# Weighted sum of gathered V rows: from one 128x128 array to four 64x64 tiles, two gathers at a time

## What is computed

```python
def block(xb):                                   # PEER_HEADS 8, PEER_TOPK 16, 16384 experts, D 1024
    ...
    best, sel = lax.top_k(cand, PEER_TOPK)
    eidx = jnp.take_along_axis(cidx, sel, axis=-1)
    gate = jax.nn.softmax(best, axis=-1)
    act = jax.nn.gelu(jnp.einsum('thkd,td->thk', u_tab[eidx], xb), approximate=False)
    return jnp.einsum('thk,thkd->td', (gate * act).astype(v_tab.dtype), v_tab[eidx])
```

## Time and profile before

| | |
|---|---|
| time, median of 3 runs | 3425.26 us (3411.93 to 3431.09) |
| the profiled execution | 3408.59 us, span 3406.8 us |
| its mean granted PE clock | 0.877 of full speed |
| busy share of the span | PE 78%, PEld 41%, DVE 45%, POOL 29%, ACT 20% |
| moved by DMA | 859.75 MB, mean 252 GB/s |
| first and last dot of layer 0's expert stage | about 930 to 1758 us |
| and of layer 1's | about 2525 to 3357 us |

### The profile page before, as it was taken

How to read it: one execution, slowest core, us unless ns; L and a number is a source line. 1 busy time by engine, 2 the same in 40 slices (tenths; PEclk the granted TensorE clock), 3 DMA queues, 4 the chain that set the end, 5 groups by cost and what they waited for, 6 DMA issues and landing times. The chain is left out here.

```text
span 3406.8 us, 25784 instructions
## 1 busy us (share of the span) xinstructions
PE 2666.7 (78%) x8145; PEld 1410.6 (41%) x8145; DVE 1542.0 (45%) x3743; ACT 697.5 (20%) x1550; POOL 994.5 (29%) x859
## 2 busy tenths in 40 slices
PE   7877778887867778777788958986857777877776
PEld 2353244445622333333336747864543333333333
DVE  0112222221276667767631434133146666666663
ACT  1113333321211212222111122120121211211211
POOL 0000043320044444444420033200014444444441
PEclk9988889898989888989989968558979989888998
DMA  6435354423299999999963301423249999999994
GB/s 215 147 101 197 106 180 153 157 96 99 83 412 414 404 395 396 409 407 419 412 276 93 120 21 38 111 62 99 81 176 405 413 407 402 399 390 400 414 407 176
DMA packets 219164, 859.75 MB, mean 252 GB/s; under 512 B 16484, under 2 KB 98877, under 8 KB 137102
## 3 DMA queue, kind: packets, MB, share of 16 engines
q0 software_dynamic: 102400, 721.47, 53.1%
q1 hardware_dynamic: 116673, 137.21, 12.6%
HBM read 845.50 MB, written 13.18 MB: 252 GB/s over the span
## 5 line engine op out<-in xcount | busy, mean ns | idle before, releaser
L1849 POOL DMA_INDIRECT exp_uv<-in_peer_uv_dram,expert x640 | 771.7, 1206 | 1331.9 <-PE exp_acc L1880 819.4
L1879 PE MATMUL exp_acc<-exp_uv,exp_diag 128*128 128x512 f32 x1280 | 744.9, 666 | 404.2 <-ACT exp_diag L1896 403.7
L1930 DVE CUSTOM_DVE_ANT_0 exp_uv<-exp_uv,htok 128x1024 f32<-128x1024 f32 x640 | 772.0, 1226 | 500.1 <-DMA exp_uv<-in_peer_uv_dram,expert 491.5
L1880 PE MATMUL exp_acc<-exp_uv,exp_diag 128*128 128x512 f32 x1280 | 709.2, 638 | 0.0
L1879 PEld LDWEIGHTS exp_acc<-exp_uv,exp_diag 128*128 128x128 f32 x1280 | 253.7, 209 | 795.7 <-ACT exp_diag L1896 531.2
L1880 PEld LDWEIGHTS exp_acc<-exp_uv,exp_diag 128*128 128x128 f32 x1280 | 266.4, 208 | 351.8 <-issue 351.8
L1888 ACT ACTIVATE exp_act<-exp_dots 128x4 f32<-128x4 f32 x160 | 32.9, 205 | 1180.2 <-DVE exp_dots L1930 1180.2
L1896 ACT ACTIVATE exp_diag<-ident,exp_w 128x128 f32<-128x128 f32 x640 | 201.8, 386 | 0.0
L501 PE MATMUL ssd_in_ps<-hT,ssd_in_w 128*128 128x320 f32 x640 | 174.9, 437 | 10.4 <-ACT hT L398 10.4
L501 PE MATMUL peer_q_ps<-hT,peer_q_w 128*128 128x320 f32 x512 | 142.9, 443 | 20.8 <-ACT hT L398 20.8
L501 PEld LDWEIGHTS ssd_in_ps<-hT,ssd_in_w 128*128 128x128 f32 x640 | 122.9, 192 | 62.5 <-issue 12.7
(11 more groups left out here) (402 smaller groups left out, 2646.7 us busy)
## 6 DMA issues: line engine op xcount, KB each, us to landing
ada_w<-in_ada_w_dram SPq DMA_DIRECT2D x12, 2048.0 KB, 7.9
attp_w<-in_ada_w_dram SPq DMA_DIRECT2D x12, 2048.0 KB, 7.8
ssd_in_w<-in_ssd_w_in_dram SPq DMA_DIRECT2D x20, 1024.0 KB, 5.3
peer_q_w<-in_peer_wq_dram SPq DMA_DIRECT2D x16, 1024.0 KB, 5.4
ab_in_w<-in_ab_w_in_dram SPq DMA_DIRECT2D x10, 1024.0 KB, 5.1
exp_uv<-in_peer_uv_dram,expert POOLq DMA_INDIRECT x640, 9.2
out_ssm_sample_dram<-state_hd SPq DMA_DIRECT2D x8, 1024.0 KB, 5.2
ssd_out_w<-in_ssd_w_out_dram SPq DMA_DIRECT2D x4, 2048.0 KB, 8.3
```

The lines of the kernel that those rows point to most:

```text
L1849: pool.indirect_dma_start(slot(g)[:], None, table, bass.IndirectOffsetOnAxis(ap=experts[:, g:g + 1], axis=0)).then_inc(landing(g)[0], 16)
L1879: pe.matmul(acc[t % 2][0][:], diag[g % (2 * GRP)][:], slot(g)[:, D:D + 512], start=False, stop=False, skip_group_check=True)
L1880: pe.matmul(acc[t % 2][1][:], diag[g % (2 * GRP)][:], slot(g)[:, D + 512:2 * D], start=False, stop=False, skip_group_check=True).then_inc( ...
L1930: dve.tensor_tensor_reduce(slot(g)[:, 0:D], slot(g)[:, 0:D], m.htok[:, t, :], 1.0, 0.0, ALU.mult, ALU.add, dots[:, i % 2, k:k + 1]).then_i ...
```

## The change

PE's work is cut otherwise; gathers, dots, weights and diagonals stay as they are. A pair of gathers g and g + 1 is now done together. Each 128x128 matmul is replaced by two of 64x64 on the diagonal blocks of `diag` (the blocks beside the diagonal are zero), with the same 512 columns. In a pair, gather g sends row half r to output partitions of half r, gather g + 1 to those of the other half, so that four consecutive matmuls use four different 64x64 tiles of the array, two row halves times two column halves. Row half r sums into its own two banks `acc[r][0]` and `acc[r][1]`. The number of matmuls per gather goes from 2 to 4, all of 512 columns.

What follows from it: PE waits for two diagonals before a pair, and `mixed` goes up by 2 after it. All four banks belong to one tile, so PE waits at the start of tiles 1 and 2 until ACT has copied all four (`okept`, 4 copies instead of 2). The copy and the waits for it move one group earlier in ACT's order. `otok` has twice the size. The sum of a token now lies in two places, and the transposes become multiplications with `fold`, 16 per tile instead of 8. The matmuls with zeros and their semaphores are gone.

```diff
-        zero = s.sb("zero", [P, P])
-        otok = s.sb("otok", [P, D])
+        otok = s.sb("otok", [P, 2, D])
...
-                pe.wait_ge(zeroed, 1)
                 def end(t):
-                    for j in range(2):
-                        pe.matmul(acc[t % 2][j][:], zero[:], m.htok[:, 0, 0:512], start=False, stop=True, skip_group_check=True).then_inc(summed, 1)
-                    pe.wait_ge(okept, 2 * t + 2)
+                    pe.wait_ge(okept, 4 * t + 4)
                     if t:
                         pe.wait_ge(added, t)
                     for c in range(KC):
-                        if t < 2:
-                            ins = pe.transpose(psT[c // 4][:, (c % 4) * P:(c % 4 + 1) * P], otok[:, c * P:(c + 1) * P], m.ident[:])
-                        else:
-                            ins = pe.matmul(psT[0][:, c * TS:(c + 1) * TS], otok[:, c * P:(c + 1) * P], m.fold[:], start=True, stop=True)
+                        for r in range(2):
+                            if t < 2:
+                                ins = pe.matmul(psT[c // 4][:, (c % 4) * P + r * TS:(c % 4) * P + (r + 1) * TS], otok[:, r, c * P:(c + 1) * P],
+                                                m.fold[:], start=True, stop=True)
+                            else:
+                                ins = pe.matmul(psT[0][:, c * TS:(c + 1) * TS], otok[:, r, c * P:(c + 1) * P], m.fold[:], start=(r == 0), stop=(r == 1))
                     ins.then_inc(oturned, 1)
                 for t in range(3):
-                    if t == 2:
-                        pe.wait_ge(okept, 2)
-                    for j in range(2):
-                        pe.matmul(acc[t % 2][j][:], zero[:], m.htok[:, 0, 0:512], start=True, stop=False, skip_group_check=True)
-                    for g in range(first[t] * TOPK, (first[t] + heads[t]) * TOPK):
-                        if t and g == first[t] * TOPK + 2 * GRP:
+                    g0_, g1_ = first[t] * TOPK, (first[t] + heads[t]) * TOPK
+                    if t:
+                        pe.wait_ge(okept, 4 * t)
+                    for g in range(g0_, g1_, 2):
+                        if t and g == g0_ + 2 * GRP:
                             end(t - 1)
-                        pe.wait_ge(diagd, g + 1)
-                        pe.matmul(acc[t % 2][0][:], diag[g % (2 * GRP)][:], slot(g)[:, D:D + 512], start=False, stop=False, skip_group_check=True)
-                        pe.matmul(acc[t % 2][1][:], diag[g % (2 * GRP)][:], slot(g)[:, D + 512:2 * D], start=False, stop=False, skip_group_check=True).then_inc(mixed, 1)
+                        pe.wait_ge(diagd, g + 2)
+                        for j in range(2):
+                            for h in range(2):
+                                for r in range(2):
+                                    q, o = slice(TS * r, TS * (r + 1)), TS * ((r + h) % 2)
+                                    ins = pe.matmul(acc[r][j][o:o + TS, :], diag[(g + h) % (2 * GRP)][q, q],
+                                                    slot(g + h)[q, D + j * 512:D + (j + 1) * 512], start=(g == g0_), stop=(g == g1_ - 2),
+                                                    skip_group_check=True)
+                        ins.then_inc(mixed, 2)
                 end(2)
...
             def _(act):
                 def end(t):
-                    for j in range(2):
-                        act.wait_ge(summed, 2 * t + j + 1)
-                        if t:
-                            act.wait_ge(oturned, t)
-                        act.copy(otok[:, j * 512:(j + 1) * 512], acc[t % 2][j][:]).then_inc(okept, 1)
+                    act.wait_ge(mixed, (first[t] + heads[t]) * TOPK)
+                    if t:
+                        act.wait_ge(oturned, t)
+                    for r in range(2):
+                        for j in range(2):
+                            act.copy(otok[:, r, j * 512:(j + 1) * 512], acc[r][j][:]).then_inc(okept, 1)
...
-                        if i == first[t] * per + 2:
+                        if i == first[t] * per + 1:
                             end(t - 1)
```

More of the change, by code:

```diff
@@ L1818, in stage_experts @@
         psT = [s.bank(f"psT{i}") for i in range(2)]
-        zeroed = s.sem("zero_ready")
         landed = m.gathered
@@ L1826, in stage_experts @@
         mixed = s.sem("mixed")
-        summed = s.sem("tile_summed")
         okept = s.sem("tile_kept")
@@ L1921, in _ @@
             def _(dve):
-                dve.memset(zero[:], 0.0).then_inc(zeroed, 1)
                 def dot(i):
```

## The result

The changed kernel takes 3479.73 us (median; 3478.64 to 3489.12), the kernel before took 3418.6 us beside it: a ratio of 1.0174, with an interval of 1.0138 to 1.021. The change makes the kernel slower by 1.7%. The profiled execution took 3478.64 us with a span of 3475.9 us, 69.1 us more than the span before, at a mean granted clock of 0.79 instead of 0.877.

A forecast was written before the change was run, and what follows sets the result against it. The transfers were taken as the bound of the expert stages. Later buffers +65, tile boundaries +4 and stage ends +3 made +72 us on 3425: 3497 us, with an 8-in-10 range of 3395 to 3565.

The forecast's parts named there:

- rival A: Expert stages: all four tiles run at once, 0.86 us per gather, time hardly moves: 3415 us, 3367 to 3450; chance 0.38.
- What bounds the kernel: Expert stages: the transfers are the bound, at 405 and 404 GB/s, 2.59 us per gather; PE needs 1.71 at full clock.
- PE late, buffer late, transfer late: Expert stages: late PE work returns buffers late and slows transfers, 421 GB/s at clock 1.00 against 375 at 0.84.
- The matmuls: PE's work per pair: today's pace kept, 3.43 us a pair, 1.71 per gather; bounds 0.86 and 3.43 per gather.
- if PE starts matmuls in program order, the next tile's first row waits behind it: Two rows per fp32 matmul: only one tile's second row and the next's first overlap, 0.43 us per matmul.
- The clock: PE's granted clock over the stages: as today, near 0.90; 0.6 to 0.8 in rival A.
- When buffers come back: First issue of a group 2.0 us later in the stages: +65 us, between 0 and +130.
- one stall lets the others in the ring catch up: Reason for the middle price of +65 us: a stall in one group lets the two others catch up.
- as many late groups again as today: Rival A's worst case within the stages: late groups through half clock, +17 us for each stage.
- Signs: PE rows and POOL: pair to pair 3.43 us, 1.71 in rival A; first issue after 4.3 us, 2.6 in rival A.
- Between tiles: Four bank copies before PE starts the next tile, 2 boundaries in 2 layers: +4 us, 0 to 10.
- The end of a stage: PE's work after the last dot: +1.5 us per layer, +3 in all; -5 per layer in rival A.

The follow-up runs named there:

- e1: The changed kernel with 4 added fp32 matmuls (128x128, 512 columns, result never read) after every second pair; 3418.91 us, ratio 0.9988 to the kernel before.
- e2: The kernel before with pairing alone: PE waits for two diagonals and counts two gathers done together, on the old 128x128 matmuls; 3593.73 us, ratio 1.0502.
- e3: The changed kernel without the second column half of v, except in each tile's first and last pair; 3383.35 us, ratio 0.9878 to the kernel before.
- e7: The changed kernel with a pair's eight matmuls reordered, both column halves on one tile before the next tile; 3487.56 us, ratio 1.021 to the kernel before.
- e6: The changed kernel with 4 added matmuls after every second pair, on 64 of the 128 array rows; 3464.88 us, ratio 1.0147 to the kernel before.
- e10: The changed kernel with only ACT's copy of a finished tile's banks moved before the next tile's second-group GELU; 3476.53 us, ratio 1.0183 to the kernel before.

## Why the prediction came out as it did

The time was forecast as 3497 us and is 3480 (+61 us between the medians), slower as expected, but by another path than the one described. That the number is near is luck: the matmuls' pace was rival A's, and A's own range, 3367 to 3450, leaves 3480 out.

*What bounds the kernel: right.* DVE's wait for landings grew (491.5 to 574.0 us), and the loss lies in the two stages with falling rate (405 and 404 to 387 and 385 GB/s). The chain "PE late, buffer late, transfer late" is the one that e1, e2 and e3 confirm from three sides.

*The matmuls: the wrong branch.* The step that failed is "if PE starts matmuls in program order, the next tile's first row waits behind it". From pair to pair it is 1.71 us, the sign named for A, not 3.43. The argument was that all rows of the trace stand in order; but these were rows of one tile, where order and a busy array can't be told apart. In the kernel after, matmuls on four tiles start within 0.02 us of each other, and e7 shows that even four rows of one tile in a row in the program hold nobody up.

The Trainium skill, "TensorE: Matmul & The Clock Gate", Part 3, says both that matmuls keep strictly to program order and that matmuls in different tiles start about 4 ns apart. The trace agrees with the second (some 7 ns at full clock); the first, applied to two rows per fp32 matmul, gave the wrong pace here. "TensorEngine Tiling (Array Packing)", Key Properties, says that different tiles can load weights and multiply in parallel, and this is what the loads in fours show.

*The clock: wrong by its condition.* "I take the clock as today" was said for two tiles at a time. e2, where PE has today's work in pairs, was granted .85 instead of .91 and .89, so it would not quite have held even there. With all four PE is busy half as long, and the stages' clock fell to 0.73 and 0.72, inside the 0.6 to 0.8 named for A. That matmuls on 64 of 128 rows bring less clock was right, as e6 shows, but wasn't needed.

*When buffers come back: right in kind, mis-sized in both branches.* The forecast had 2.0 us later at the first issue for +65 us. e2, the same mechanics alone, measured 2.55 us more lateness for 179 us over both layers; at that rate 2.0 us would be 140, above even the upper end of 130. The reason given, that one stall lets the others in the ring catch up, is what fell: the time from issue to dot did not shrink (10.26 to 10.31 us, 10.00 in e2). The reading behind it, that two or three gathers are under way, was low as well: by the trace of before it is 3.6 in the mean, and 9.2 / 2.49 from the earlier trace rows is 3.7. In A the worst case was "as many late groups again as today", +17 per layer, a figure without a working. Measured were 148 late groups instead of 42. With this count the prediction's own rows give the right size: 106 more groups at 1.8 us each make 1.19 us over 160 groups, with 0.3 for the second diagonal 1.5 us (measured 1.36), and at 26.7 turns 40 us per layer, +80.

*Signs.* From PE's start to POOL's first issue I named 4.3 us for the forecast and 2.6 for A. It is 3.99 at the median, near the wrong one: A's pair at half clock takes as long as the forecast's at full clock. The stages' rates, 387 and 385 GB/s, are near the 389 named for the forecast too. These signs didn't tell the cases apart; the distance of the matmuls' starts did.

*Between tiles:* +4 us was taken, at most 10. In the changed kernel e10's traces show 6.5 us and its time nothing; with the clock held up it is 14.1 us over 4 boundaries in the traces, more than the upper end.

*The end of a stage:* +1.5 per layer in the forecast, -5 in A; measured -4.7 and -3.1.

So the sum is A's mechanism with the full price of lateness: +77.8 in the stages, -7.8 at their ends, +70.0 against 69.1 of span. The forecast's +72 came from a path that is not there (no cost from slower pairs) with a price that was too low, and the two errors met.

## What to carry to other kernels

Where a ring of buffers feeds a transfer-bound stage, the time that counts is from "data used up" to "buffer reissued", and each microsecond of it was paid here about once per turn of the ring; count the turns before calling a delay covered, and see whether the time from issue to use shrinks. Making a bursty TensorE faster can make it later: compare its rest before each burst with before, and if the granted clock falls, add idle matmuls to hold it, which here won 1.1% on the old kernel too. Release a buffer as soon as its own work is done, and drain what the next tile needs before the work that waits for it.

## What the hardware showed that was not expected

- Four 64x64 tiles run fp32 matmuls of 512 columns fully side by side: 16 rows in 1.71 us at full clock, 3.4 at half, in either order of the program (e7).
- Matmuls that only fill time raise the granted clock of a stage from 0.73 to 0.90 (four per group) and 0.97 (six), and on the kernel before from 0.91 to 0.98 (two per group). Over 64 of the array's 128 rows four of them reach only 0.82, at a busier PE.
- A clock of 0.60 goes with 408 GB/s when the buffers are free early (e3), and 0.85 with 365 when they are not (e2): clock and rate are tied through the kernel's waits, not directly. The Trainium skill, "TensorE: Matmul & The Clock Gate", Part 1, on oscillation, says that a wait for data between bursts of matmuls brings the clock back to half. The trace agrees: in the changed kernel 148 of 160 groups begin at half clock, and the median rest before a group is 4.9 us.
